# Four of a norm's seven additions on GpSimd instead of VectorE, in five stages of a three-layer transformer kernel

## What is computed

```
def rms_norm(x, w):
    xf = x.astype(jnp.float32)
    y = xf * lax.rsqrt(jnp.mean(xf * xf, axis=-1, keepdims=True) + EPS)
    return (y * w.astype(jnp.float32)).astype(x.dtype)
...
    for layer in range(DEPTH):
        h = rms_norm(x, norm_mix_pre[layer])
        m = mixer_block(h, ...)
        x = x + rms_norm(m, norm_mix_post[layer]).astype(x.dtype)
        h = rms_norm(x, norm_ffn_pre[layer])
        f = swiglu(h, w_ffn_gate[layer], w_ffn_up[layer], w_ffn_down[layer])
        x = x + rms_norm(f, norm_ffn_post[layer]).astype(x.dtype)
```

## Time and profile before

| | |
|---|---|
| median of 3 runs | 2559.23 us (2558.46 to 2559.93) |
| the profiled execution's own time | 2559.72 us |
| its span in the profile | 2557.9 us |
| granted TensorE clock over the span | 0.999 |
| TensorE busy | 2525.1 us |
| VectorE busy | 1916.7 us |
| ScalarE busy | 1328.2 us |
| GpSimd busy | 56.6 us, 59 instructions |
| DMA | 266.23 MB, mean 104 GB/s |

### The profile page before, as it was taken

How to read it: one execution, slowest core, us unless ns; L and a number is a source line. 1 busy time by engine, 2 the same in 40 slices (tenths; PEclk the granted TensorE clock), 3 DMA queues, 4 the chain that set the end, 5 groups by cost and what they waited for, 6 DMA issues and landing times.

```text
span 2557.9 us, 42180 instructions
## 1 busy us (share of the span) xinstructions
PE 2525.1 (99%) x17164; PEld 2323.6 (91%) x17164; DVE 1916.7 (75%) x2723; ACT 1328.2 (52%) x2008; POOL 56.6 (2%) x59
## 2 busy tenths in 40 slices
PE   9999999999999999999999999999999999999998
PEld 8888999999989888999989998999989777999987
DVE  6956888688954795688788993698945798698954
ACT  5345644556633534654465572455633467556631
POOL 0020000000000003000000000000000000000000
PEclk9999999999999999999999999999999999999999
DMA  4242332333333324243333334233333430233332
GB/s 157 83 117 81 124 108 83 124 124 108 101 112 93 116 83 138 60 124 116 116 111 104 108 98 116 77 124 117 101 110 104 116 104 2 75 124 113 101 109 83
DMA packets 77216, 266.23 MB, mean 104 GB/s; under 512 B 9600, under 2 KB 12032, under 8 KB 76128
## 3 DMA queue, kind: packets, MB, share of 16 engines
q1 hardware_dynamic: 71136, 254.87, 32.5%
q10 hardware_dynamic: 5888, 8.68, 1.3%
HBM read 251.71 MB, written 4.19 MB: 100 GB/s over the span
## 4 chain that ended last, share of the span: by engine, by line
PE 77%; DVE 16%; ACT 3%; issue 3%; DMA 1%; ACTq 0%; DVEq 0%; SPq 0%
PE bank L517 23%; PE bank L519 23%; PE bank L518 23%; DVE w_lo L750 2%; PE bank L2124 1%; PE bank L2102 1%; DVE acc L862 1%; DVE x L919 1%; DVE u_lo L848 1%; PE bank L2088 1%; DVE w_lo L1292 1%; DVE lev_q L2588 1%; PE bank L1851 1%; DMA raw<-in_weights 1%; DVE ffn_out L910 1%
## 5 line engine op out<-in xcount | busy, mean ns | idle before, releaser
L517 PE MATMUL bank<-u_hi,w_hi 128*128 128x256 f32 (+1 forms) x2352 | 739.7, 315 | 5.0 <-DVE w_lo L750 3.2
L519 PE MATMUL bank<-u_hi,w_lo 128*128 128x256 f32 (+1 forms) x2352 | 728.3, 310 | 0.0
L518 PE MATMUL bank<-u_lo,w_hi 128*128 128x256 f32 (+1 forms) x2352 | 728.3, 310 | 0.0
L750 DVE TENSOR_TENSOR w_lo<-raw,w_hi 128x1024 fp32r<-128x1024 f32 x250 | 311.0, 1248 | 309.4 <-ACT w_hi L746 309.2
L517 PEld LDWEIGHTS bank<-u_hi,w_hi 128*128 128x128 f32 x2352 | 449.0, 191 | 34.7 <-DVE w_lo L750 7.4
L518 PEld LDWEIGHTS bank<-u_lo,w_hi 128*128 128x128 f32 x2352 | 449.2, 191 | 23.1 <-issue 2.6
L519 PEld LDWEIGHTS bank<-u_hi,w_lo 128*128 128x128 f32 x2352 | 449.2, 191 | 21.0
L746 ACT ACTIVATE w_hi<-raw 128x1024 fp32r<-128x1024 f32 x250 | 262.8, 1053 | 312.5 <-PE bank L519 222.8
L517 PE MATMUL bank<-cm,w_hi 128*128 128x256 f32 x1152 | 317.1, 275 | 2.0 <-DVE hid_f L1260 2.0
L518 PE MATMUL bank<-cm,w_hi 128*128 128x256 f32 x1152 | 316.8, 275 | 0.0
L519 PE MATMUL bank<-cm,w_lo 128*128 128x256 f32 x1152 | 316.8, 275 | 0.0
(11 more groups left out here) (358 smaller groups left out, 4365.3 us busy)
## 6 DMA issues: line engine op xcount, KB each, us to landing
raw<-in_weights SPq DMA_DIRECT2D x314, 512.0 KB, 3.5
rx<-in_weights SPq DMA_DIRECT2D x72, 512.0 KB, 3.5
xr<-in_weights SPq DMA_DIRECT2D x48, 512.0 KB, 3.6
raw<-in_weights SPq DMA_DIRECT2D x32, 384.0 KB, 3.1
rot_s<-rot_in ACTq DMA_DIRECT2D x32, 128.0 KB, 2.4
q_s<-q_in ACTq DMA_DIRECT2D x52, 64.0 KB, 3.4
x<-in_x SPq DMA_DIRECT2D x4, 512.0 KB, 6.7
ret_mask<-in_ret_mask SPq DMA_DIRECT2D x2, 1024.0 KB, 6.4
```

What stands on the lines that cost most here:

```text
L517: nc.tensor.matmul(out, st_hi, mv_hi, start=first, stop=False, skip_group_check=onto)
L518: nc.tensor.matmul(out, st_hi, mv_lo, start=False, stop=False, skip_group_check=onto)
L519: return nc.tensor.matmul(out, st_lo, mv_hi, start=False, stop=last, skip_group_check=onto)
L750: nc.vector.tensor_tensor(w_lo[:, bl.slot(p), :], raw[:, bl.raw(p), :], w_hi[:, bl.slot(p), :].bitcast(F32), ALU.subtract).then_inc(lo_spl ...
```

## The change

In stages 1, 3, 4, 5 and 6 GpSimd does the first four of the seven additions (`pool_squares`), with the same waits: for the square and for the addition before it. VectorE starts with the fifth (`first=POOL_SQUARES + 1`), which waits for the fourth by `acc_done`. Stages 0 and 2 stay as they were. GpSimd's calls stand in its queue behind the rotary work of each layer: stage 1 or 3 ahead of the wait for the whole `x` of stage 2 or 4, and stages 4, 5 and 6 behind the last of these waits.

```
+POOL_SQUARES = 4
+POOL_STAGES = (1, 3, 4, 5, 6)
...
+        def pool_squares(pool, s):
+
+            for k in range(1, POOL_SQUARES + 1):
+                pool.wait_ge(sq_done.sem, sq_done.upto(s, k + 1))
+                if k > 1:
+                    pool.wait_ge(acc_done.sem, acc_done.upto(s, k - 1))
+                nc.gpsimd.tensor_tensor(acc[:, :], sq_x[:, K_ORDER[0], :] if k == 1 else acc[:, :], sq_x[:, K_ORDER[k], :],
+                                        ALU.add).then_inc(acc_done.sem, 1)
+
-        def dve_squares(dve, s, order=K_ORDER):
+        def dve_squares(dve, s, order=K_ORDER, first=1):
 
-            for k in range(1, KD):
+            for k in range(first, KD):
...
             if more:
                 dve_split(dve, bl, p + 3)
-                dve_squares(dve, s + 1)
+                dve_squares(dve, s + 1, first=POOL_SQUARES + 1 if s + 1 in POOL_STAGES else 1)
...
             dve_split(dve, bl, p + KD + 3)
-            dve_squares(dve, s + 1)
+            dve_squares(dve, s + 1, first=POOL_SQUARES + 1)
...
+                pool_squares(pool, 2 * li + 1)
                 pool.wait_ge(x_ready.sem, x_ready.upto(li * 2 + 2, 2 * KD))
+            for s in (4, 5, 6):
+                pool_squares(pool, s)
```

## The result

| | before | after |
|---|---|---|
| median | 2559.45 us (5 runs, 2558.46 to 2559.93) | 2574.09 us (5 runs, 2573.01 to 2574.72) |
| ratio | 1 | 1.0057 [1.0045, 1.0068] |
| span of the profiled execution | 2557.9 us | 2572.6 us |
| mean granted TensorE clock | 0.999 | 0.996 |

What follows compares the result with a forecast made beforehand. TensorE, busy 99% of 2557.9 us, was taken as the bound. 4 x 3.0 + 1.3 + 0.6 = 13.9 us on 2559.72 gave 2573.6, with the median 0.5 lower: 2573 us, range 2563 to 2578.

Steps and rivals of the forecast that it cites:

- One addition holds VectorE for 1.09 us: In the joins, each GpSimd addition stops VectorE's two-SBUF-input instructions for 1.09 us; bounds 0.43 and 1.28 us.
- rival (a): VectorE's 128x256 join instructions run beside GpSimd unheld; TensorE wins 0.98 us in four stages: 2555.3 us; chance 0.10.
- The other price weighed: Pricing a GpSimd addition by the spacing of starts, 1.23 us; a whole stage would lose 0.6 us more.
- The two alternate, GpSimd first: In the join, GpSimd waits for VectorE's instruction under way, then VectorE's next one waits: one instruction each.
- Rival (b): GpSimd gets its turn only where VectorE has nothing to issue; additions follow w_lo: 12 us, 2571.2 us; chance 0.05.
- Four additions ahead of the fifth `u_lo`: Joins into stages 1, 3, 5, 6: all four GpSimd additions precede the fifth u_lo, delaying it 4.36 us to 507.26.
- 3.0 us a stage in 1, 3, 5, 6: In these four joins the sum of acc starts 3.0 us later, at 515.2 in place of 512.22.
- hold, less slack, less the vanished wait for `acc`: Loss per join in stages 1, 3, 5, 6: 4.36 us held, less 0.4 of slack, less 0.98 that vanishes.
- TensorE waits about 4 us a stage for `u_lo`: Sign expected in the trace of stages 1, 3, 5, 6: TensorE waiting for u_lo, about 4 us per stage.
- The wait for `acc` gone, stage 4 excepted: TensorE no longer waits for acc in stages 1, 3, 5, 6; stage 4 still does, its sum 1.3 us later.
- 0.6 us more on `hid_f`: Feed-forwards after stages 1, 3, 6: r comes 0.2 us later than TensorE, adding 0.6 us of waiting for hid_f.

Runs made afterwards that it cites:

- The memsets: The changed kernel with GpSimd's four additions per stage replaced by memsets of acc, same waits and signals: 2552.94 us, 0.9978 of the kernel before.
- the wait filled: The changed kernel with six unused 512-column matmuls in TensorE's long wait for u_lo in stages 1, 3, 5 and 6: 2571.46 us, 1.0049.
- moving the sum: The kernel before, with the matmul that sums acc ahead of k = 7 of block 3 instead of k = 6, in all seven norms: 2558.26 us, 0.9997.

## Why the prediction was right

The time, 2574.09 us, is 1.1 above the 2573 forecast and inside the range, and the mechanism is the one forecast. By its steps:

- **One addition holds VectorE for 1.09 us: right.** 1.07 on instructions of 128x256, 1.08 on `w_lo`. That no row showed GpSimd beside such short instructions was the main doubt, and rival (a), no hold on them, fell by four spans of 1.5 us in place of 0.45. The memsets show that reading SBUF is what does it. The other price weighed, the spacing of GpSimd's starts (the Trainium skill, Perfetto Trace Analysis, GPSIMD Engine Instruction), 1.23 us, is too high for this; VectorE loses less than GpSimd's instruction lasts.
- **The two alternate, GpSimd first: right**, but for the first addition. Rival (b), in which GpSimd comes last, fell: that addition started at 499.77, amid VectorE's instructions. The VectorE instruction that began after it, at 500.10, still took 0.42 us; only the one at 500.43 was held.
- **Four additions ahead of the fifth `u_lo`: wrong in detail.** Three came ahead of it. The second and third stood together and held the work ahead of the fourth `u_lo`, and so the long wait, 1.94 us, was for the fourth. The fifth square (ready at 505.81) was so late that the fourth addition (505.90) came after the fifth `u_lo` (505.75) and made the sixth late. TensorE at full clock waits for that one, 0.82 us with the wait filled; slowed, it arrived after it. The end of the join did not change by this, since all four lie ahead of the sixth `u_lo`.
- **3.0 us a stage in 1, 3, 5, 6: undersized.** It was 3.42, 3.40, 3.43 and 3.41 (by the join itself; 3.55 from `r` to `r`). The term that was missing is TensorE's lower clock after the long wait, 0.37 us as a mean of the four joins profiled; with the wait filled a join cost 3.04. The working of hold, less slack, less the vanished wait for `acc` was therefore right to 0.1 us.
- **TensorE waits about 4 us a stage for `u_lo`: wrong as a sign to look for.** It waited 2.3 us (0.37 and 1.94). The delay of block 3 was there, 511.96 - 0.14 - 507.35 = 4.5 us against 4.0 in the forecast. The rest of it, which the list of waits does not show, is some 1.6 us of slow matmuls (16 x 0.10) and 0.5 us in the first, slower steps after each wait.
- **The wait for `acc` gone, stage 4 excepted: right**, and stage 4 lost 1.66 us ahead of and in `w_lo` (forecast 1.7), and 1.20 us at `r` (forecast 1.3).
- **0.6 us more on `hid_f`: wrong, by sign.** I put `r` 0.2 us later than TensorE because ScalarE's copies would be. It came 1.28 us after the sum's start, not later than before (1.35), and waited 0.18 us for it. The wait for `hid_f` fell by 0.5 us, in stage 1; why it had been longer there before is not shown.
- **The sum.** 4 x 3.45 + 1.2 - 0.5 + 0.1 = 14.6 instead of 4 x 3.0 + 1.3 + 0.6 = 13.9. A term too small by 1.8 and one too large by 1.1 nearly cancelled: part of the closeness is luck.

## What to carry to other kernels

An idle GpSimd is not free capacity: while VectorE works with two SBUF inputs, each GpSimd instruction that reads SBUF takes VectorE's time, so price it by what the waiting VectorE instruction loses, and look at what VectorE is doing where it falls, not only at the chain that is to be relieved. Before work is moved to another engine, look at the spacing of a dependent chain: two partial sums in turn took the whole wait away with no other engine. And when a wait is removed, ask which later one waits for the same result: moving the sum showed that the wait for `acc` and the one for `hid_f` are both waits for `r`.

## What was not expected of the hardware

- After a wait of 1.94 us in the middle of a join TensorE was mostly granted 1.2 GHz for about 3.5 us, and 0.87 of the clock over the 13 us of the window. Matmuls put into the wait kept it at 2.4 GHz. It fell in nine of the twelve joins, of three kernels, with such a wait and nothing in it, and stayed at 2.4 GHz in the other three; what decides is open.
- A GpSimd copy of 128x512 holds VectorE for 0.41 us, an addition of the same size for 1.07, a memset not at all.
- VectorE's additions of 128x512 start 0.60 us apart if each depends on the last but one, and 0.78 to 0.80 if on the last.
